# Nested expert loops with a shorter last prefetch, first maxima in two sets of heads, bias sums by VectorE, and stores awaited behind the barrier

## The reference

```python
h = rms_norm(x, attn_norm_w[layer])
proj = h @ w_in[layer]
(fq, fk, fv, ff, mq, mk, mv, mi, mf, mo) = jnp.split(proj, split_at, axis=-1)
...
fox_y = head_group_norm(forgetting_attention(fq, fk, fv, fox_log_f), fox_out_norm_w[layer])
mlstm_y = head_group_norm(m_h, mlstm_out_norm_w[layer]) * jax.nn.sigmoid(mo)
x = x + jnp.concatenate([fox_y, mlstm_y], axis=-1) @ w_out[layer]
h2 = rms_norm(x, moe_norm_w[layer])
top_v, top_i = lax.top_k(h2 @ router_w + router_b, 4)      # 32 experts
gates = jax.nn.softmax(top_v, axis=-1)
x = x + sum of gate * (act(h2 @ w_gu[e] + b_gu[e]) @ w_down[e] + b_down[e])
```

## Time and profile before

| | us |
|---|---|
| three runs | 2175.14, 2176.84, 2182.24 |
| median | 2176.84 |
| the profiled execution | 2182.6 |
| its span | 2180.9 |

### The profile page before, as it was taken

One profiled execution on the slowest core, in us unless ns is written; L12 is line 12 of the kernel. 1 busy time (PEld: TensorE's weight loads), 2 busy tenths in 40 slices (PEclk: granted clock), 3 DMA queues, 4 the chain that ended last, 5 costly groups with the idle time before them and its releaser, 6 DMA issues.

```text
span 2180.9 us, 39001 instructions
## 1 busy us (share of the span) xinstructions
PE 2104.2 (96%) x11205; PEld 1814.9 (83%) x11206; DVE 1597.7 (73%) x2121; ACT 1274.1 (58%) x1631; POOL 911.1 (42%) x909
## 2 busy tenths in 40 slices
PE   7999999999997999999999999999999999999996
PEld 6877777865886998888998899899887899889895
DVE  4555662553337778898878987888998888898876
ACT  4245342545235667676666766666776766776664
POOL 2015762244564234445334533433546443543532
PEclk9999998799996999999999999999999999999998
DMA  5233455303245779899877987987999987998976
GB/s 187 76 92 109 138 141 143 101 1 103 86 147 197 258 261 356 271 383 388 272 260 255 375 295 262 349 270 258 369 384 376 389 282 260 362 388 289 357 260 213
DMA packets 290264, 543.26 MB, mean 249 GB/s; under 512 B 39400, under 2 KB 51653, under 8 KB 290212
## 3 DMA queue, kind: packets, MB, share of 16 engines
q1 hardware_dynamic: 267972, 486.17, 66.1%
q0 software_dynamic: 22240, 56.42, 6.9%
HBM read 509.34 MB, written 44.14 MB: 254 GB/s over the span
## 4 chain that ended last, share of the span: by engine, by line
PE 75%; DVE 2%; DMA 2%; issue 2%; ACT 1%; POOL 0%; SPq 0%; DVEq 0%; POOLq 0%; ACTq 0%
PE banks L2634 17%; PE banks L208 11%; PE banks L210 11%; PE banks L209 11%; PE banks L2636 7%; PE banks L2011 3%; PE banks L2570 2%; PE banks L2569 2%; PE banks L1295 2%; DMA RAW<-in_expert_w_gate_up 1%; PE banks L2633 1%; PE banks L1997 1%; PE banks L1996 1%; DVE VL L1274 1%; PE banks L1973 1%
## 5 line engine op out<-in xcount | busy, mean ns | idle before, releaser
L1274 DVE TENSOR_TENSOR VL<-RAW,VH 128x2048 fp32r<-128x2048 f32 x389 | 882.2, 2287 | 28.8 <-ACT VH L1269 23.2
L1269 ACT ACTIVATE VH<-RAW 128x2048 fp32r<-128x2048 f32 x390 | 733.7, 1910 | 111.6 <-PE banks L210 76.3
L2634 PE MATMUL banks<-T,VH 128*128 128x384 f32 x1920 | 542.1, 357 | 2.5 <-DVE T L1315 2.5
L2636 PE MATMUL banks<-T,VL 128*128 128x192 f32 x1680 | 422.1, 251 | 0.0
L2634 PEld LDWEIGHTS banks<-T,VH 128*128 128x128 f32 x1920 | 345.8, 190 | 3.4 <-issue 2.9
L2636 PEld LDWEIGHTS banks<-T,VL 128*128 128x128 f32 x1680 | 321.6, 191 | 0.5
L2329 POOL DMA_INDIRECT out<-yb,ycur x32 | 78.3, 2447 | 413.0 <-DVE yb L2473 395.8
L209 PE MATMUL banks<-VL,T 128*128 128x512 f32 x544 | 211.9, 390 | 0.0
L208 PE MATMUL banks<-VH,T 128*128 128x512 f32 x544 | 211.9, 390 | 0.0
L210 PE MATMUL banks<-VH,T 128*128 128x512 f32 x544 | 211.8, 389 | 0.0
L208 PE MATMUL banks<-VH,A 128*128 128x512 f32 x512 | 204.1, 399 | 4.5 <-DVE A L2453 3.3
(11 more groups left out here) (391 smaller groups left out, 4070.1 us busy)
## 6 DMA issues: line engine op xcount, KB each, us to landing
RAW<-in_expert_w_gate_up SPq DMA_DIRECT2D x528, 512.0 KB
RAW<-in_expert_w_down SPq DMA_DIRECT2D x262, 512.0 KB
RW<-in_w_in SPq DMA_DIRECT2D x24, 512.0 KB, 5.8
xin<-in_x SPq DMA_DIRECT2D x8, 512.0 KB, 11.4
MBC<-dM SPq DMA_DIRECT2D x8, 512.0 KB, 11.1
dQ<-parts SPq DMA_DIRECT2D x8, 512.0 KB, 3.0
dK<-parts SPq DMA_DIRECT2D x8, 512.0 KB, 3.0
WRAW<-in_w_out SPq DMA_DIRECT2D x8, 512.0 KB, 8.3
```

The source lines that it names most:

```text
L1269: act.activation(VH[:, i, ks], RAW[:, i, ks], ACT.Copy).then_inc(s_hi, 1)
L1274: dve.tensor_tensor(VL[:, i, ks], RAW[:, i, ks], VH[:, i, ks].bitcast(f32), ALU.subtract).then_inc(s_w, 1)
L2634: last = pe.matmul(o[:, 0:2 * NW], VH[:, c % 3, k, col], T2[:, k], start=k == 0, stop=k == KT - 1)
L2636: pe.matmul(o[:, HI_ALL], VL[:, c % 3, k, col], T2[:, k, HI_ALL], start=False, stop=False)
```

## The change

1. In block 1 VectorE makes the low parts of the next kind's weights before `normed` of the last tile, no longer after it.
2. SP no longer waits at the end of block 1 for its stores. In block 2 SP waits for them after the loads of tiles 3 and 4 and before those of the values, and POOL before its fill of VT. SP loads the values of tiles 0 to 3 before dC and the hots.
3. The first maxima come in two sets of four heads: six groups ahead of the units on two pairs of banks, six behind units 2, 3, 5, 6, 8 and 10. Heads 4 to 7 of tiles 0 to 3 are turned behind units 0 to 3. The later maxima stand behind units 12 to 27, one each. The eight matmuls of line 2025 are gone. POOL fills part of the ones in QA.
4. VectorE adds the down bias from PSUM to `x1` itself; ScalarE's copies and POOL's sums are gone.
5. The expert loop is nested, rounds of eight turns, with a test before each round and each turn. SP runs the same loop; its table `turns` is gone. Three and a half chunks are loaded ahead instead of five and a half.

```diff
@@ block 1, VectorE's piece loop
                     for hf in range(2):
                         piece(*slot(2 * u + hf))
-                        if hf == 0 and last in NORMED:
-                            normed(last)
                         if j == TT - 1 and n + 1 < len(KINDS):
                             split_lo(n + 1, 2 * hf)
                             split_lo(n + 1, 2 * hf + 1)
+                        if hf == 0 and last in NORMED:
+                            normed(last)
@@ end of block 1, SP
-                for i in range(SR):
-                    sp.wait_ge(s_sent[i], 16 * len([y for y in STAGED[i::SR] if y not in NORMED]))
@@ groups, units
-    GROUPS = [(t, h, n) for t, n in ((0, 8), (1, 4), (2, 2), (3, 2)) for h in range(0, H, n)]
+    HALF = H // 2
+    GROUPS = [(t, h0 + h, n) for h0 in (0, HALF) for t, n in ((0, 4), (1, 4), (2, 2), (3, 2)) for h in range(0, HALF, n)]
+    NOW = len(GROUPS) // 2
+
+    def group_pair(g):
+        return g % 2 if g < NOW else 0
...
     def maxima_after(u):
         if u < 28:
-            return range(4 * u // 7, 4 * (u + 1) // 7)
+            return range(max(0, u - 12), max(0, u - 11))
         return range(16 + (u - 28) // 2, 17 + (u - 28) // 2) if u < 60 and u % 2 == 0 else range(0)
 
+    def group_after(u):
+        return {2: 6, 3: 7, 5: 8, 6: 9, 8: 10, 10: 11}.get(u)
+
+    PREPS = {0: (0, 3), 1: (1, 3), 2: (2, 3), 3: (3, 3), 4: (4, 2), 5: (4, 3)}
+    PREPS.update({u: (5 + n // 4, n % 4) for n, u in enumerate((8, 10, 11, 12, 14, 15, 16, 17, 18, 19, 20, 21))})
...
     def rows_after(u):
-        return {8: 4, 15: 5, 22: 6, 29: 7, 36: 8, 44: 9, 52: 10, 60: 11}.get(u)
+        return {5: 4, 6: 5, 9: 6, 12: 7, 17: 8, 21: 9, 25: 10, 29: 11, 36: 12, 44: 13, 52: 14, 60: 15}.get(u)
...
+    def turn_bank(n):
+        return ps[4 + n % 4] if n < 8 else ps[6 + n % 2]
@@ block 2, SP
             tile(3)
             tile(4)
+            all_stored(sp)
+            for t in range(4):
+                values_tile(t)
             sp.dma_start(KA[CROW:CROW + 2, :, CH:S].bitcast(f32), dC[:, :, CH:S]).then_inc(s_aug, 16)
             sp.wait_ge(s_hots, 1)
             for h in range(H):
                 sp.dma_start(KA[MROW:STK, h].bitcast(f32).rearrange("p (r c) -> p r c", c=P), bc(hots[MROW:STK, h].unsqueeze(1), [2 * H, TT, P])).then_inc(s_aug, 16)
...
             def finished(u):
-                sp.wait_ge(s_xo, u + 1)
+                sp.wait_ge(s_yd, 2 * u + 2)
...
-            sp.wait_ge(s_w, 2)
-            load(sp, 3, 0)
+            sp.wait_ge(s_w, 1)
+            load_half(sp, 3, 0, 0)
@@ block 2, POOL
+            all_stored(pool)
+            link(pool.memset(VT[:, :, :, HD:VA], 1.0))
+            pool.memset(QA[CROW:CROW + 2, 0, HALF:H].bitcast(f32), 1.0).then_inc(s_ones, 1)
+            pool.wait_ge(s_ones, 1)
...
+            pool.wait_ge(s_vt, TT)
+            pool.wait_ge(s_T, TURN_OF["prep", 2, 3] + 1)
+            pool.memset(QA[CROW:CROW + 2, 1].bitcast(f32), 1.0).then_inc(s_ones, 1)
...
-            def biased(u):
-                pool.wait_ge(s_yd, 2 * u + 2)
...
-                pool.tensor_tensor(x1[:, u % XB], x1[:, u % XB], yd[:], ALU.add).then_inc(s_xo, 1)
@@ block 2, ScalarE
-            def bias_out(u, c, bank):
-                act.wait_ge(s_gb, 2 * u + c + 1)
...
-                act.activation(yd[:, c * CH:(c + 1) * CH], bank, ACT.Copy).then_inc(s_yd, 1)
@@ block 2, VectorE
             for t in range(4):
-                dve.memset(QA[CROW:CROW + 2, 0, :, tok(t)].bitcast(f32), 1.0).then_inc(s_one, 1)
+                dve.memset(QA[CROW:CROW + 2, 0, 0:HALF, tok(t)].bitcast(f32), 1.0).then_inc(s_one, 1)
...
-            dve.memset(QA[CROW:CROW + 2, 1].bitcast(f32), 1.0).then_inc(s_one, 1)
...
+            def biased(u, c, bank):
+                dve.wait_ge(s_gb, 2 * u + c + 1)
...
+                x = x1[:, u % XB, c * CH:(c + 1) * CH]
+                dve.tensor_tensor(x, x, bank, ALU.add).then_inc(s_yd, 1)
...
+                if t >= 3:
+                    biased(t - 3, 0, ps[5])
+                    biased(t - 3, 1, ps[5])
                 residual(t, 0)
...
+            for c in range(2):
+                biased(TT - 3, c, ps[c])
             route(last)
...
+            for c in range(2):
+                biased(TT - 2, c, ps[2 + c])
+            for c in range(2):
+                biased(TT - 1, c, ps[c])
             split_lo(dve, 0, 0, 1)
...
-            ahead = rank[0:1].rearrange("a t e -> a (t e)")[:, 0:SSB]
-            link(dve.tensor_scalar(ahead, iotaU[0:1, 0:SSB], se[0:1, NE - 1:NE], -float(SSB), ALU.add, ALU.add))
-            dve.tensor_scalar(turns[:], ahead, 0.0, None, ALU.max).then_inc(s_turns, 1)
@@ block 2, PE
-            for i in range(8):
-                pe.matmul(ps[5], KA[0:HD, 0, tok(0)], KA[0:HD, 0, 0:CH], start=True, stop=True)
+            for t in range(3):
+                prepare(t, 2)
             pe.wait_ge(s_const, 1)
...
+            for g in range(NOW):
+                maxima_of_group(g)
+                if g == 1:
+                    prepare(3, 2)
+                if g in (2, 3):
+                    rows(g - 2)
...
+                if group_after(u) is not None:
+                    maxima_of_group(group_after(u))
                 for m in maxima_after(u):
                     maximum(m)
@@ the expert loop, every engine
-            with eng.Fori(0, SSB) as s:
-                with eng.If(s < n):
+            with eng.Fori(0, TURNS_ALL, ROUND) as first:
+                with eng.If(first < n):
+                    with eng.Fori(0, ROUND) as i:
+                        s = first + i
+                        with eng.If(s < n):
+                            turn(s)
+                        with eng.Else():
+                            eng.nop()
@@ the expert loop, SP
                 for c in range(NCH):
-                    wait(s_w, s * N2 + (2 * (c + 2) + 2))
-                    load_half(sp, (c + 5) % NCH, e if c == 0 else en, 1)
-                    wait(s_w, s * N2 + (2 * (c + 3) + 1))
-                    load_half(sp, c, en, 0)
...
-            with sp.Fori(0, SSB) as turn:
-                with sp.If(turn + n >= SSB):
-                    weights(sp.value_load(turns[0:1, bass.ds(turn, 1)], min_val=0, max_val=SSB - 1))
...
+                    wait(s_w, s * N2 + 2 * (c + 1))
+                    load_half(sp, (c + 3) % NCH, e if c < 3 else en, 1)
+                    wait(s_w, s * N2 + 2 * (c + 1) + 1)
+                    load_half(sp, (c + 4) % NCH, e if c < 2 else en, 0)
+
+            n = superblocks(sp, weights)
```

231 lines of the change are left out of this document (103 added, 128 removed).

## The result

The change makes the kernel faster by less than was forecast: the median is 2166.47 us (ten runs, 2159.91 to 2173.34) against 2181.11 us for the kernel before in ten runs, a ratio of 0.9933, interval 0.9921 to 0.9945. That is 14.6 us where 25.7 were forecast, and the time lies 0.5 us above the end of the range. The profiled execution after took 2167.42 us with a span of 2165.8, 15.1 less than the span before.

The account below looks back on a forecast made before the run. TensorE bounds the expert stretch; gains lie where it waits or runs at half clock. Terms 4 + 1.6 + 7.7 + 2.6 + 9.8 = 25.7 us, off 2176.8, give 2151.1 us; range 2141 to 2166, forecast case alone 2144 to 2160.

Parts of the forecast that it names:

- A: Block 1: splits moved ahead of `normed` start earlier and shorten PE's wait for weights; 4 us gain, 1 to 6.5.
- B: Barrier between the blocks: SP no longer waits for its stores, so PE's drain is last; 1.6 us gain.
- C: Start of block 2: first maxima in two sets bring scores 18.8 us earlier; net gain 7.7 us, 2 to 14.
- margin of 3 us for the hots: Start of block 2: hots land at 382 us, scores ready at 385.5, so their loading stays hidden.
- D: Routing tables and tile loop: VectorE adds the bias, removing 5.2 us of long steps; net 2.6 us, -1 to 5.
- E: Kernel end: nested expert loops leave three empty rounds instead of 21 empty turns; 9.8 us gain, 6 to 11.
- The expert stretch: 701 to 2161 us: PE busy 1454.9 of 1460 us, idle 5.1, so no gain or loss was entered.
- the clock stays down in the first units: Rival, attention units 0 to 10: mixed maxima and transposes keep PE at 1.2 GHz; +16 us, 2167, chance 0.11.
- The attention loop gives it all back: Rival, units 2 to 27: late VectorE work makes each unit wait 0.3 us; 8 us, 2159, chance 0.06.
- nested loop costs at each turn: Rival, expert loop: 0.3 us falls on PE in each of 32 turns; 9.9 us, 2161, chance 0.05.

Follow-up runs that it names:

- e6: The changed kernel with all four splits of the next weights ahead of `normed` and the second mLSTM piece; 2167.21 us, ratio 0.9943.
- e5: The changed kernel with the stores' wait also at the end of block 1, as before the change; 2166.75 us, ratio 0.9939.
- e2: The changed kernel with the first half of chunk 3 loaded only after two splits, as before the change; 2159.94 us, ratio 0.9902.
- e14: The kernel before with only the nested loops, three and a half chunks ahead and chunk 3 after one split; 2175.52 us, ratio 0.9983.
- e16: The changed kernel with chunk 3 after two splits, dC and hots before the values, first expert-weight split behind the small table chain; 2158.57 us, ratio 0.9899.
- e15: The changed kernel with ScalarE's copies and POOL's bias sums restored and chunk 3 loaded after two splits; 2161.68 us, ratio 0.9919.
- e4: The changed kernel with a flat loop of 53 turns on every engine instead of the nested one; 2175.08 us, ratio 0.9973.
- e13: The changed kernel unaltered, run again beside three other kernels on one chip; 2164.34 us, ratio 0.9929.
- e3: The changed kernel with the four last bias sums behind the first split of the expert weights; 2165.06 us, ratio 0.9922.
- e11: The changed kernel with chunk 3 after two splits, dC and hots before the values, four last bias sums behind the first expert-weight split; 2162.35 us, ratio 0.9935.

## Why the prediction was wrong

**A, 4 us forecast, nothing measurable.** This is the step that failed first. "Moved ahead of `normed` they can start when the buffer is there" was right, and so was 2.8 us for the two splits undisturbed (2.66). What was wrong is that the wait of 4.0 us was then the gain. The second pair of splits stood at the same place as before, and behind it the mLSTM's chain. I had read one wait of PE and not what PE would wait for next. I had also seen that the first pair took 2.1 us too long, but not asked what held it: it lay beside POOL's products. With the splits gone from there the small `den` steps lie beside them and are held instead, 2.5 us, and POOL's root comes later. e6 takes away both of PE's waits for WL and gives the time to PT and `num`. The clock was not won either: it was 0.50 from 244 to 250, where it had been from 240 to 246.

**B, 1.6 forecast.** The barrier came as forecast, right behind PE's drain. In the stretch table A and B together are 0.8 us, since the end of PE's work in block 1 was itself 0.8 later. e5 shows no difference in time.

**C, 7.7 forecast, 9.4 in the profiles.** 21.5 us were won before the first scores, where 18.8 were forecast, and 12.1 given back, for 11.1. The surplus is the clock, as I read it: I had priced the whole start at 1.2 GHz, and its first eight microseconds ran at 2.4. That part of the gain was luck. The margin of 3 us for the hots was not there, because the rest had become faster: before the first scores PE stood still 1.84 us, and 0.68 in the builds that load the hots first.

**D, 2.6 forecast, -1.2 in the profile, with E in it.** The 5.2 us in VectorE's long steps are gone as forecast, and the four sums behind the list take 2.47 us, near the 2.8 forecast. But the half of them that I took to be hidden is not: PE waits 5.4 us for `diag` where it waited 3.0, so 2.4 are on the path instead of 1.4. Before the last routing PE waits 2.0 us for `x1`, where 1.4 were forecast. What I missed beside that stands further down the queue. E's load of chunk 3 after one split, for which the sum has no term, sets 512 KB loads beside the gather of the first rows. That is 2.7 us of the stretch (e2), and it happens on the kernel before as well (e14, 1.5 us). The first split now lies over POOL's gather, which it lengthens by 1.75 us; e16 shows 0.7 of the stretch in it. Without the early load D is worth 1.8 us (e15 against e2).

**E, 9.8 forecast, 10.1 in the profile at the end,** and nothing a turn from the nesting. Its price for the tables is the one above. In the timed runs E is less sure: taken away from the change it costs 8.6 us (e4), put alone on the kernel before it brings 1 to 7 (e14), and the traces do not say why the two differ.

**The expert stretch, 0 forecast.** It took 3.7 us more in the change's profile, 1.7 in e13 and less than before in five of the other builds. Most of what differs lies in the five narrow turns in which the DMA engines are busy all the time, so that I put it down to the arrival of the weights; no run varies that alone. The prediction had no term for such a draw.

By the two profiles, of the 10.5 us that are missing 4.8 are A and B, 3.8 are the tables, 3.7 the experts in that execution, 0.2 the tile stage, less 1.7 and 0.3 that C and E brought more.

Of the rivals, "the clock stays down in the first units" did not come: the clock is 0.90 from 384 to 400, 1.00 from 390 on. The Trainium skill's sentence that the full clock does not engage for transposes ("TensorE: Matmul & The Clock Gate", section "Part 4: PE-mode transpose") is not borne out by this trace as a rule for a mixed stretch: from 369 to 377 the clock is 1.00 with twelve transposes at the start and the small matmuls of the maxima behind them. "The attention loop gives it all back" did not come: PE waits 1.4 us for `nmax` of the later maxima (1.9 before) and 2.0 for QB, and 12.1 us are given back in all. The "nested loop costs at each turn" did not come either (0.1 us in 18 turns).

At POOL's fill the trace shows what the prediction had no row for: the cast of 374.40 was held until the fill ended, 1.10 us instead of 0.17, within the 0 to 1 us that was counted. The Trainium skill's rule of a pair of ports that VectorE and GpSimd share and that is locked for a whole instruction ("SBUF — State Buffer", section "SBUF: two separate sides") agrees with that; the places where holding cost time were others, the divisions in block 1 and the gather. The gather's instruction on POOL goes from 1.32 to 3.07 us beside a VectorE split with two operands in SBUF, in all twelve builds that have them side by side, and is 1.32 in e3, e11, e15 and e16, which have not, as in the kernel before and e14. The sums with an operand in PSUM, directly ahead of it, are not shown to hold anything.

## What to carry to other kernels

Before a wait is entered as a gain, look at what the waiting engine needs next, and when that is ready; A's wait came back one step later, first for the second pair and then, in e6, under another name. When a step takes longer than its size, ask what lies beside it on the other engines, and what will lie there after the move. When a step is moved, go through the queue behind it down to the transfers: a load that is allowed 1 split earlier cost 2.7 us because it met a small gather that everything waited for. Loops over a bound on the number of turns are worth nesting where the skipped turns stand at the end: 18 of them were 10 to 11 us of the profiled end here, and the second loop cost nothing that could be seen.

## What the runs showed of the hardware that was not expected

- After a stop of PE of 1.3 us at the barrier the clock stayed at 1.00 for the next five to eight microseconds, in all fifteen builds that have that stop. In the three that have one of 2.9 us it fell to 0.50 between just ahead of PE's first turn (before, e5) and 2 us behind it (e14), and in e5 it came back for some three microseconds.
- Small VectorE steps that started beside a POOL instruction ended with it in three places: 1.63 us instead of 0.15 (`den`, block 1), 2.22 instead of 0.18 (routing tables, before), 1.10 instead of 0.17 (a cast beside a fill).
- A POOL instruction that issues an indirect DMA takes 3.07 us instead of 1.32 when a VectorE subtraction with both operands in SBUF runs beside it (twelve builds).
- Marks move by 1 to 4 us from build to build where the edit does not reach them, and the same program's from one profile to the next (the change and e13, 369.0 and 367.1 us for block 2): over the builds block 2 begins between 366.9 and 371.3 us, and five narrow expert turns take 194.0 to 198.6 us. Terms of a sum that are smaller than this need more than one profile.
